# The first stage of a two-block transformer kernel: table load, warm-up products, and the first norm's sums of squares

## The reference, cut to what matters

```
h    = x * rsqrt(mean(x*x, axis=-1) + 1e-6) * attn_norm_w
proj = h @ w_in            # 2048 x 8192, split into eight parts of 1024 columns
```

## Time and profile before

| | us |
|---|---|
| median of three runs | 2481.05 (2480.87 to 2483.22) |
| the profiled execution, its own time | 2483.36 |
| its span in the trace | 2481.6 |
| TensorE busy | 2469.2 |
| VectorE busy | 1750.1 |
| ScalarE busy | 1192.9 |

### The profile page before, as it was taken

How to read it: one execution, slowest core, us unless ns; L and a number is a source line. 1 busy time by engine, 2 the same in 40 slices (tenths; PEclk the granted TensorE clock), 3 DMA queues, 4 the chain that set the end, 5 groups by cost and what they waited for, 6 DMA issues and landing times.

```text
span 2481.6 us, 29559 instructions
## 1 busy us (share of the span) xinstructions
PE 2469.2 (100%) x11904; PEld 2167.5 (87%) x11904; DVE 1750.1 (71%) x2158; ACT 1192.9 (48%) x1465; POOL 26.8 (1%) x27
## 2 busy tenths in 40 slices
PE   9999999999999999999999999999999999999999
PEld 8898888888888888888888888888888888888888
DVE  6887788788888888886566565467688855555555
ACT  6545544544444444445665554444544444444443
POOL 0000000000000000000010000000000000000000
PEclk9999999999999999999999999999999999999999
DMA  8656666788788888886455455555488756555554
GB/s 334 237 189 235 221 209 249 257 317 305 284 304 299 304 301 301 292 306 236 151 185 173 155 172 196 202 190 189 173 297 293 286 188 205 202 202 204 189 204 150
DMA packets 82632, 582.37 MB, mean 235 GB/s; under 512 B 9409, under 2 KB 9793, under 8 KB 12609
## 3 DMA queue, kind: packets, MB, share of 16 engines
q1 hardware_dynamic: 82352, 580.38, 66.1%
q10 hardware_dynamic: 144, 0.12, 0.0%
HBM read 578.36 MB, written 2.10 MB: 234 GB/s over the span
## 4 chain that ended last, share of the span: by engine, by line
PE 97%; DVE 1%; DMA 1%; issue 1%; ACT 0%; SPq 0%; POOL 0%; POOLq 0%; ACTq 0%
PE bank L851 30%; PE bank L853 30%; PE bank L852 30%; PE bank L561 2%; PE bank L641 1%; DMA raw<-in_w_in_dram 1%; PE bank L679 0%; DVE wlo L1274 0%; PE bank L690 0%; PE bank L691 0%; PE bank L660 0%; PE bank L649 0%; PE bank L659 0%; PE bank L680 0%; PE bank L702 0%
## 5 line engine op out<-in xcount | busy, mean ns | idle before, releaser
L1274 DVE TENSOR_TENSOR wlo<-raw,whi 128x1024 fp32r<-128x1024 f32 x886 | 1080.6, 1223 | 633.0 <-ACT whi L882 628.1
L882 ACT CAST whi<-raw 128x1024 fp32r<-128x1024 f32 x886 | 928.1, 1049 | 916.0 <-PE bank L853 890.1
L851 PE MATMUL bank<-whi,hH 128*128 128x512 f32 x2528 | 970.8, 384 | 0.4 <-DVE wlo L1274 0.2
L853 PE MATMUL bank<-whi,hL 128*128 128x512 f32 x2528 | 958.6, 379 | 0.0
L852 PE MATMUL bank<-wlo,hH 128*128 128x512 f32 x2528 | 958.6, 379 | 0.0
L853 PEld LDWEIGHTS bank<-whi,hL 128*128 128x128 f32 x2528 | 478.1, 189 | 68.0
L851 PEld LDWEIGHTS bank<-whi,hH 128*128 128x128 f32 x2528 | 478.4, 189 | 67.4 <-issue 1.2
L852 PEld LDWEIGHTS bank<-wlo,hH 128*128 128x128 f32 x2528 | 478.5, 189 | 65.2
L1701 DVE SCALAR_TENSOR_TENSOR adacc<-raw,stat,adacc 128x512 f32<-128x512 f32 x360 | 269.8, 749 | 6.8
L851 PE MATMUL bank<-whi,aH 128*128 128x512 f32 x704 | 267.4, 380 | 0.0
L852 PE MATMUL bank<-wlo,aH 128*128 128x512 f32 x704 | 266.8, 379 | 0.0
(11 more groups left out here) (295 smaller groups left out, 1424.0 us busy)
## 6 DMA issues: line engine op xcount, KB each, us to landing
raw<-in_w_gu_dram SPq DMA_DIRECT2D x176, 1024.0 KB, 5.0
raw<-in_w_ada_dram SPq DMA_DIRECT2D x96, 1024.0 KB, 5.0
raw<-in_w_down_dram SPq DMA_DIRECT2D x88, 1024.0 KB, 4.9
raw<-in_w_in_dram SPq DMA_DIRECT2D x62, 1024.0 KB, 4.9
raw<-in_w_in2b_dram SPq DMA_DIRECT2D x56, 1024.0 KB, 4.8
raw<-in_w_out_dram SPq DMA_DIRECT2D x32, 1024.0 KB, 4.8
raw<-in_w_in2a_dram SPq DMA_DIRECT2D x8, 1024.0 KB, 4.8
raw<-in_w_mla_dram SPq DMA_DIRECT2D x8, 1024.0 KB, 4.8
```

The source lines that it names most:

```text
L851: e.matmul(o, xh[:, kt, sl], pairs(wh, i), start=k == 0, stop=False)
L853: ins = e.matmul(o, xl[:, kt, sl], pairs(wh, i), start=False, stop=k == n - 1)
L882: e.copy(whi[i][:, :, :], raw[u % RAW][:, 2 * hf:2 * hf + 2, :]).then_inc(*ev("act_hi", c, 0))
L1274: e.tensor_tensor(wlo[i][:, :, :], raw[u % RAW][:, 2 * hf:2 * hf + 2, :], f(whi[i][:, :, :]), ALU.subtract).then_inc(*ev("dve_lo", c, 0))
```

## The change

1. ScalarE does a copy of one column of `stat` right behind the issue of `vec`, before it waits for that transfer.
2. The opening products of ones have 512 columns in place of 128, and there are 16 in place of 30.
3. `x0` and its two transfers are gone, and with them the eight squares with accumulation in slots 9 to 12. In their place ScalarE squares `xT` from SBUF, in eight instructions of 512 columns (two feature tiles each): three in slot 4, three in slot 5, two in slot 6, ahead of the high half of that slot. VectorE adds the eight tiles of squares with seven additions of 512 columns and one of 256 (one in slot 5, three in slot 6, four in slot 7). TensorE sums over the partitions in slot 8 with two products whose moving operand is one column of ones, and VectorE copies the two columns out and takes the mean in slot 8. The side work of block 0 is put off by 2 slots instead of 6. The identity matrix is loaded at u = 5.

```
-WARM = 30
+WARM = 16
@@ shared
+        SQ = T + AD[:1]
@@ late0
-            return 6 if b.index == 0 else 0
+            return 2 if b.index == 0 else 0
@@ TensorE, side_work(s)
+                if s == 8:
+                    e.wait_ge(*on("dve_x0", "halves"))
+                    o = next_bank(e, "x0")
+                    for m in range(2):
+                        ins = e.matmul(o[:, m:m + 1], SQ[0][:, P * m:P * m + P], f(ones_r[:, 0:1]), start=True, stop=True)
+                    ins.then_inc(*ev("pe_x0"))
@@ TensorE, beginning
-                e.matmul(banks[7][:, 0:P], ones_r[:, :], ones_r[:, :], start=True, stop=True)
+                e.matmul(banks[7][:, :], ones_r[:, :], ones_r[:, :].unsqueeze(1).to_broadcast([P, 4, P]), start=True,
+                         stop=True)
@@ ScalarE, side_work(s)
-                if 9 <= s < 13:
-                    m, q = (s - 9) // 2, (s - 9) % 2
-                    if q == 0:
-                        e.wait_ge(sem_x0[m], 16)
-                    for j in (2 * q, 2 * q + 1):
-                        ins = e.activation((T + AD[1:])[4 * m + j][:, :], x0[:, m, 512 * j:512 * j + 512], ACT.Square, bias=0.0,
-                                           scale=1.0, accum_out=sc(ssq + 4 * m + j))
-                    if s == 12:
-                        ins.then_inc(*ev("act_x0"))
+                for i in {4: (0, 1, 2), 5: (3, 4, 5), 6: (6, 7)}.get(s, ()):
+                    e.activation(SQ[i][:, :], xT[:, 2 * i:2 * i + 2, :].rearrange("p a b -> p (a b)"), ACT.Square,
+                                 bias=0.0, scale=1.0).then_inc(*ev("act_x0", i))
@@ ScalarE, beginning
             e.dma_start(vec[:, :], a["vec"]).then_inc(sem_vec, 16)
+            e.wait_ge(*on("dve_half"))
+            e.activation(sc(b_warm), sc(b_half), ACT.Copy, bias=0.0, scale=1.0)
             e.wait_ge(sem_vec, 16)
@@ VectorE, side_work(s): squares_of_x(s), behind small(s)
+                def add(o, i, name):
+                    e.tensor_tensor(o, o, i, ALU.add).then_inc(*ev("dve_x0", name))
+
+                if s == 5:
+                    e.wait_ge(*on("act_x0", 1))
+                    add(SQ[0][:, :], SQ[1][:, :], "0+1")
+                elif s == 6:
+                    e.wait_ge(*on("act_x0", 3))
+                    add(SQ[2][:, :], SQ[3][:, :], "2+3")
+                    e.wait_ge(*on("act_x0", 5))
+                    add(SQ[4][:, :], SQ[5][:, :], "4+5")
+                    e.wait_ge(*on("dve_x0", "2+3"))
+                    add(SQ[0][:, :], SQ[2][:, :], "0..3")
+                elif s == 7:
+                    e.wait_ge(*on("act_x0", 7))
+                    add(SQ[6][:, :], SQ[7][:, :], "6+7")
+                    e.wait_ge(*on("dve_x0", "6+7"))
+                    add(SQ[4][:, :], SQ[6][:, :], "4..7")
+                    e.wait_ge(*on("dve_x0", "4..7"))
+                    add(SQ[0][:, :], SQ[4][:, :], "all")
+                    e.wait_ge(*on("dve_x0", "all"))
+                    add(SQ[0][:, 0:S], SQ[0][:, S:2 * S], "halves")
+                elif s == 8:
+                    e.wait_ge(*on("pe_x0"))
+                    e.tensor_copy(sc(b_r1, 2), side("x0")[:, 0:2]).then_inc(*side_free("x0"))
+                    e.wait_ge(*side_read("x0"))
                     mean(("r1",), b_r1, 2, D)
@@ SyncE
-                elif u in (5, 7):
-                    m = (u - 5) // 2
-                    e.dma_start(x0[:, m, :], a["x"][:, m, :]).then_inc(sem_x0[m], 16)
-                    if u == 7:
-                        e.dma_start(ident[:, :], a["ident"]).then_inc(sem_ident, 16)
+                elif u == 5:
+                    e.dma_start(ident[:, :], a["ident"]).then_inc(sem_ident, 16)
```

More of the change, by code:

```diff
@@ L348, in two_block_kernel @@
         xT = at("xT", [P, KT, S], F32, mix_at)
-        x0 = at("x0", [P, 2, D], F32, mix_at + 16 * KB)
         Qx = at("Qx", [P, 2, 1024], F32, x_at)
@@ L466, in two_block_kernel @@
         sem_xT = [sem(f"s_xT{i}") for i in range(6)]
-        sem_x0 = [sem(f"s_x0{m}") for m in range(2)]
         sem_x1, sem_vec, sem_late, sem_pos = sem("s_x1"), sem("s_vec"), sem("s_late"), sem("s_pos")
@@ L484, in sc @@
             return stat[:, b:b + n]
-        b_half = cols(16)
+        b_half, b_warm = cols(16), cols(1)
         b_c, b_e, b_lb, b_om = cols(16), cols(16), cols(16), cols(16)
@@ L1320, in small, with squares_of_x @@
                     ins.then_inc(*ev("dve_sel"))
[L1321 to L1325, removed]
+            def squares_of_x(s):
+                def add(o, i, name):
[23 more added lines that the diff above has]
+                    e.wait_ge(*side_read("x0"))
                     mean(("r1",), b_r1, 2, D)
@@ L1881, in side_work @@
                 small(s)
+                squares_of_x(s)
                 for b, t in live(s):
```

## The result

| | before | after |
|---|---|---|
| median of five runs, us | 2481.05 (2480.87 to 2483.22) | 2491.49 (2491.09 to 2493.98) |
| the profiled execution, its own time | 2483.36 | 2491.09 |
| span | 2481.6 | 2489.3 |

The changed kernel is slower, ratio 1.004 with a 95% interval of 1.003 to 1.0051. The page first: busy time, then the chain by engine.

What follows compares the result with a forecast made beforehand. TensorE, busy 2469.2 of 2481.6 us, was taken to bound the kernel. A wait of 8.8 us plus 1.6 for slow products gave 10.4, so 2491.4 from the median of 2481.05; range 2485.5 to 2496.5.

Steps and rivals of the forecast that it cites:

- What bounds the start: Until 25.17 us the kernel waits for bytes, so the start's possible 2.85 us (1.28 + 1.57) was costed at zero.
- the stated sign for this step: At the start: chunk 6 still within 0.3 us of 25.2, with a longer TensorE wait ahead of it.
- Nothing moves the landing of unit 3: Start: unit 3, issued at 7.64, lands at 22.73 whatever ScalarE or TensorE does; chunk 6 starts at 25.17 again.
- ScalarE: Slots 4 to 6: squares at 0.53 us each put chunk 8's high half at 30.36 to 31.39, before 27.68.
- VectorE: Slots 5 to 7: additions behind chunk 8's low half at 31.42 end with "halves" at 38.95 us.
- TensorE's two products: Slot 8: two small products with their weight loads cost 0.3 us, bounds 0.1 and 0.8.
- The wait in sum: Ahead of chunk 8: TensorE waits for the sums, starting at about 39.3 instead of 30.46, 8.8 us.
- The clock after the wait: First products of chunk 8 run slow after the idle time: 1.57 us, bounds zero and 3.1.
- Sum: Whole kernel: 8.8 + 1.6 = 10.4 us slower, 2491.4 us with the median of before.
- A: Start's gain comes through, 2.85 us off, and the sums are hidden: 2478.2 us; chance 0.05.
- B: Nothing moves: VectorE reaches "halves" close to when TensorE reaches slot 8, 2480 to 2482 us; chance 0.06.
- D: More loss: additions at 0.75, clock low twice as long, a slow norm stretch lengthens: 2497 to 2501 us; chance 0.09.

Runs made afterwards that it cites:

- the new start alone: Kernel before with only the table load moved and 16 opening products of 512 columns: 2481.86 us against 2481.44, ratio 1.0002.
- the last experiment's second kernel: Kernel before plus products of ones (512 columns) at the norms, 8 before the second half's turns, 3 before the product behind them: 2481.32 us, ratio 0.9997.
- products of ones in the wait: Changed kernel with 30 products of ones (512 columns) in slot 8 ahead of the wait for the sums: 2490.34 us, ratio 1.0034.
- all sums late: Changed kernel with squares in slots 7 to 10, additions in 8 to 12, products with ones and mean in 13: 2482.8 us against 2482.5, ratio 1.0002.
- the sums alone: Changed kernel with the old start (table load behind the transfers, 30 products of 128 columns): 2492.09 us, ratio 1.0042.
- the late small tables: Changed kernel with squares, additions and products in later slots, and `posi` and `freq` issued at u = 10: 2482.51 us, ratio 1.0.

## Why the prediction was right

- *What bounds the start.* Right in what it costs: parts 1 and 2 came to nothing, alone and in the changed kernel. Of the 2.85 us TensorE had 2.37 at the end of chunk 0 (9.34 against 11.71): the 16 products of ones took 5.83 us and not 5.0, so block 0 began at 6.75 and not near 6.3. The step was mis-placed in its detail. I held chunk 6 to 25.17 by unit 3; it started at 24.66 and waited for nothing. The waits were ahead of chunks 1 and 4. So it was the earlier transfers that took the saving, and the stated sign for this step (chunk 6 within 0.3 us of 25.2, with a longer wait ahead of it) failed. At chunk 8 nothing of the saving can be told: 30.21 with the new start alone, 30.00 with the old start in the last experiment's second kernel.
- *"Nothing moves the landing of unit 3"*, 22.7. Nothing in the change does, but it isn't a constant. It was 20.98 in the profile of after and 20.3 to 23.9 over all. The 8.8 us hung on it one for one: 1.75 less in this execution.
- *ScalarE.* From chunk 6's high half to chunk 8's I had 7.55 (22.81 to 30.36); it was 7.47 (21.06 to 28.53). A square costs 0.52 (three from 22.82 to 24.38), against the 0.53 that I took.
- *VectorE.* From chunk 8's low half to the end of "halves" I had 7.53 (31.42 to 38.95); it was 7.56 (29.59 to 37.15). Sums of durations from near rows were good to 0.1 us.
- *TensorE's two products.* 0.3 predicted, 0.87 measured (37.20 to 38.07), above the upper bound of 0.8 and, for its size, the term furthest off in the chain. They are four instructions, each with a weight load, and they ran at the slow clock; at full clock they took 0.47 (products of ones in the wait) and 0.37 (all sums late, 43.20 to 43.57).
- *The wait in sum.* 8.8 less 1.75 for the landing, plus 0.57 for the products, is the 7.6 measured.
- *The clock after the wait.* 1.57 predicted, 2.36 measured. The products were slow for 4.7 us and not for 3.1. The bounds held it; the products of ones in the wait showed the cause. The size is luck of the execution: with the sums alone it was 1.46 behind nearly the same wait (4.05 less 2.59).
- *Sum.* 10.4 predicted, 9.97 at chunk 9, 10.4 between medians. Two of the errors cancel: the landing (-1.75) against the products and the clock (+0.57, +0.79). So the median came closer (2491.4 against 2491.49) than the terms were; that last step is luck, since the landing and the clock both differ from execution to execution.
- *The rivals.* A is out by the start alone and by the sums alone. B would be right with all sums late, and shows what was wrong with the change: the slots, not the sums. Of D the clock came half way, 2.36 between 1.57 and 3.1; the additions took 0.70 to 0.72 and not 0.75, and no slow stretch at a norm was there in this profile.

## What to carry to other kernels

A sum off the busy engine's path still costs if its last step stands in that engine's queue: ask in which slot the engine reaches it, and whether the feeding engines can have it done by then. Work that "fits beside" another engine fits only in a stretch where that engine is the bound; here slots 4 to 7 were the stretch in which ScalarE and VectorE were catching up with the transfers, and three to five slots later the same work cost nothing that could be told. And a saving ahead of a transfer that ends later is none.

## What the runs showed of the hardware

- An idle time of 7.2 us cost 2.4 us more on the products of chunk 8 and 0.4 on the small ones: the record has the granted clock at 0.50 from 32.5 to 42.7 us, the last 5.5 us of it over products (37.2 to 42.7). With the sums alone, behind 7.05 us, it was at 0.50 from 33.8 to 40.6, and chunk 8 lost 1.5.
- Two idle times of 1.86 and 0.88 us at a norm brought 3.4 us at 0.50 in some executions and none in others, 1.1 to 1.2 us each time; in the profile of the late small tables it was 6.8 us at the first norm. With the waits filled the upper 8 of 21 runs of before have no counterpart, so this is most of its spread.
- In the first microseconds the granted clock is shown as 1.00 while products of 512 columns take 0.63 us, the length that goes with 0.50 elsewhere. There the durations are to be believed. 30 products of 128 columns over 6.5 us left it so the earlier trace rows; the first real products behind 16 of 512 columns took 0.38 at once.
- The 16 products of ones took 5.28 to 6.64 us in eight profiles of the same instructions: the moment at which the clock rises differs from execution to execution.
- The fourth unit of the queue (unit 3) landed between 20.7 and 23.9 us in nine profiles that issued the same bytes ahead of it, and at 20.3 and 21.4 in the two that issued the small tables later. What scatters it stays open.
